# Second attention: queries split per head and 128 tokens, the low part subtracted by GpSimd

## What is computed

```python
def gqa_attend(q, k, v):
    s = jnp.einsum('bkgqd,bksd->bkgqs', q, k, preferred_element_type=jnp.float32) * (HEAD_DIM ** -0.5)
    p = jax.nn.softmax(s, axis=-1).astype(v.dtype)
    return jnp.einsum('bkgqs,bksd->bkgqd', p, v)
...
    o_blocks = lax.map(lambda qb: gqa_attend(qb, k_all, v_all), q_blocks)
...
    o_c = gqa_attend(queries(h_ctx), k_c, v_c)
```

## Time and profile before

| | us |
|---|---|
| median of 3 runs | 3610.65 |
| lowest and highest | 3608.27, 3615.75 |
| the profiled execution, its own time | 3610.93 |
| its span in the trace | 3609.1 |
| TensorE busy | 3254.8 (90%) |
| VectorE busy | 1550.9 (43%) |
| ScalarE busy | 1124.5 (31%) |
| GpSimd busy | 535.9 (15%) |

### The profile page before, as it was taken

The page is one execution under the profiler, slowest core; times in us unless marked ns, Lnnn a source line. Parts: engine busy times, 40 slices in busy tenths (PEclk is TensorE's granted clock), DMA queues, the critical chain, the costliest instruction groups (busy, mean ns, idle before and its releaser), DMA issues. The chain is left out here.

```text
span 3609.1 us, 48582 instructions
## 1 busy us (share of the span) xinstructions
PE 3254.8 (90%) x19154; PEld 2431.0 (67%) x19154; DVE 1550.9 (43%) x2410; ACT 1124.5 (31%) x1679; POOL 535.9 (15%) x394
## 2 busy tenths in 40 slices
PE   7997957999998899988787989999998999899998
PEld 5665611576466687867566778886556888748877
DVE  5644178243224666222655332220006887723332
ACT  4213153142113333233555332220004544422321
POOL 0000022000103343250122220000004322100001
PEclk9998978999999999989798889999997999889999
DMA  3564110121230222211000011111112111112222
GB/s 132 201 250 169 59 38 0 70 95 47 94 128 24 93 94 79 89 66 65 1 1 1 24 47 70 70 47 48 50 68 75 55 69 71 51 67 93 97 84 88
DMA packets 30566, 267.90 MB, mean 74 GB/s; under 512 B 2864, under 2 KB 5296, under 8 KB 10160
## 3 DMA queue, kind: packets, MB, share of 16 engines
q1 hardware_dynamic: 30384, 265.36, 20.0%
HBM read 261.15 MB, written 4.19 MB: 74 GB/s over the span
## 5 line engine op out<-in xcount | busy, mean ns | idle before, releaser
L632 PE MATMUL banks<-normed_high,weights_high 128*128 128x512 f32 (+1 forms) x2264 | 842.0, 379 | 84.6 <-DVEq L455 47.5
L632 PE MATMUL banks<-normed_low,weights_high 128*128 128x512 f32 (+1 forms) x2264 | 831.4, 375 | 0.0
L632 PEld LDWEIGHTS banks<-normed_high,weights_high 128*128 128x128 f32 x2264 | 437.3, 193 | 192.3 <-ACT weights_high L542 41.5
L632 PE MATMUL banks<-normed_high,weights_low 128*128 128x512 f32 (+1 forms) x2264 | 544.5, 371 | 0.0
L263 DVE TENSOR_TENSOR weights_low<-ring,weights_high 128x1024 fp32r<-128x1024 f32 (+1 forms) x194 | 269.5, 1389 | 607.3 <-ACTq L555 539.2
L632 PEld LDWEIGHTS banks<-normed_low,weights_high 128*128 128x128 f32 x2264 | 438.9, 194 | 73.1 <-issue 1.2
L632 PEld LDWEIGHTS banks<-normed_high,weights_low 128*128 128x128 f32 x2264 | 405.2, 191 | 73.7
L553 ACT ACTIVATE weights_high<-ring 128x1024 fp32r<-128x1024 f32 (+1 forms) x226 | 260.9, 1154 | 618.1 <-PE banks L632 452.5
L587 POOL TENSOR_TENSOR latent_total<-latent_total,latent_square 128x512 f32<-128x512 f32 x42 | 77.1, 1836 | 1441.9 <-ACTq L530 1441.9
L632 PE MATMUL banks<-ffn_hidden,ring 128*128 128x256 f32 (+1 forms) x704 | 227.3, 486 | 1.1 <-PEq L154 1.1
L2830 PE MATMUL banks<-normed_high,hg_weights_high 128*128 128x512 f32 (+1 forms) x512 | 190.1, 371 | 15.1 <-DVEq L455 15.1
(11 more groups left out here) (539 smaller groups left out, 4787.9 us busy)
## 6 DMA issues: line engine op xcount, KB each, us to landing
ring<-in_ffn_up SPq DMA_DIRECT2D x33, 2048.0 KB, 7.5
ring<-in_ada SPq DMA_DIRECT2D x48, 1024.0 KB, 6.4
ring<-in_ffn_down SPq DMA_DIRECT2D x24, 1408.0 KB, 5.9
ring<-in_hgrn SPq DMA_DIRECT2D x16, 1536.0 KB, 6.4
ring<-in_gates SPq DMA_DIRECT2D x6, 2048.0 KB, 8.1
ring<-in_wo SPq DMA_DIRECT2D x6, 2048.0 KB, 8.0
ring<-in_w_rw SPq DMA_DIRECT2D x5, 1536.0 KB, 7.5
ring<-in_branch SPq DMA_DIRECT2D x3, 2048.0 KB, 7.8
```

The lines of the kernel that those rows point to most:

```text
L632: mm = pe.matmul(ps[:, 0:y.shape[-1]], w, y, start=(not sweep and kk == 0 and n == 0), stop=(sweep != 0 and kk == kt - 1 and n == len(pair ...
```

## The change

`pa_queries` becomes a ring of 8 pieces, each one head's 128 queries (one unit). ScalarE rounds the piece of unit u+4 in round u, behind its copy of unit u-1, in one 64x128 instruction; it waits until the score of the unit that used the piece's place before is done. GpSimd does the subtraction, also per unit: the pieces of units 0 to 3 first, then the piece of unit u+3 ahead of the probabilities' product of unit u, after its product of unit u-1 has landed. Before the product it waits for its own subtraction. TensorE's score waits for `queries_parted` in every unit. VectorE has nothing to do with the queries any more. `high` and `low` are as before.

```diff
+QUERIES_AHEAD = 4
...
-        QS = k.sb("pa_queries", [P, 2, 2, L], s, F32R)
+        QS = k.sb("pa_queries", [P, 2 * QUERIES_AHEAD, P], s, F32R)
...
+        def queries(u):
+            g, p, j, qt, t, cols, keys = of(u)
+            return Q[rows(p), t, cols.start + qt * P:cols.start + qt * P + P]
...
-                    if qt == 0 and p == 0:
-                        pe.wait_ge(parted.sem, parted.at(j + 1))
+                    pe.wait_ge(parted.sem, parted.at(u + 1))
...
-                    q = QS[:, j % 2, p, qt * P:qt * P + P]
+                    q = QS[:, u % (2 * QUERIES_AHEAD), :]
...
-                def part(j):
...
-                    v.wait_ge(rounded.sem, rounded.at(j + 1))
-                    for p in range(2):
-                        v.tensor_tensor(QS[rows(1 - p), j % 2, p, 0:w], Q[rows(p), t, cols],
-                                        QS[rows(p), j % 2, p, 0:w].bitcast(F32), ALU.subtract).then_inc(e.sem, e.tick())
-                    v.wait_ge(e.sem, e.now())
-                    v.sem_inc(parted.sem, 1)
-                part(0)
-                part(1)
...
-                    if u < n_units and units[u] == (first_group[groups[units[u][0]][0]], 1):
-                        j = groups[units[u][0]][0]
-                        if 1 <= j and j + 1 < n_pairs:
-                            part(j + 1)
...
+                def part(u):
+                    p, x = units[u][1], u % (2 * QUERIES_AHEAD)
+                    g.wait_ge(rounded.sem, rounded.at(u + 1))
+                    g.tensor_tensor(QS[rows(1 - p), x, :], queries(u), QS[rows(p), x, :].bitcast(F32),
+                                    ALU.subtract).then_inc(parted.sem, 1)
+                    g.wait_ge(parted.sem, parted.at(u + 1))
+                for u in range(QUERIES_AHEAD):
+                    part(u)
                 for u in range(n_units):
+                    if u and u + QUERIES_AHEAD - 1 < n_units:
+                        g.wait_ge(normed.sem, normed.at(u))
+                        part(u + QUERIES_AHEAD - 1)
                     x = slice(u % 4, u % 4 + 1)
                     probs = PB[:, u % 3, 0:of(u)[6]]
...
-                def part(j):
...
-                    if j >= 2:
-                        a.wait_ge(scored.sem, scored.at(2 * last_group[j - 2] + 2))
-                    for p in range(2):
-                        a.activation(QS[rows(p), j % 2, p, 0:w], Q[rows(p), t, cols], ACT.Copy).then_inc(e.sem, e.tick())
-                    a.wait_ge(e.sem, e.now())
-                    a.sem_inc(rounded.sem, 1)
+                def part(u):
+                    p, x = units[u][1], u % (2 * QUERIES_AHEAD)
+                    if u >= 2 * QUERIES_AHEAD:
+                        a.wait_ge(scored.sem, scored.at(u - 2 * QUERIES_AHEAD + 1))
+                    a.activation(QS[rows(p), x, :], queries(u), ACT.Copy).then_inc(rounded.sem, 1)
...
-                    if u < n_units and units[u] == (first_group[groups[units[u][0]][0]], 1):
...
+                    if u + QUERIES_AHEAD < n_units:
+                        part(u + QUERIES_AHEAD)
```

12 lines of the change are left out of this document (2 added, 10 removed).

## The result

| | before | after |
|---|---|---|
| median, us | 3611.87 | 3590.15 |
| lowest, highest of the 6 runs after, us | | 3586.78, 3598.61 |
| ratio, with its 95% interval | | 0.9948 (0.9935 to 0.9960) |

The ratio stands for 18.8 us less (14.4 to 23.5); it leaves out one slow run of before (4577.98 us), and likewise one of "before, wide split later" (7833.19). The prediction was 3584.3 us in a range of 3574 to 3602, so 26.3 us less. A second measurement of the same kernel gave 3592.42 us and 0.9950 (0.9931 to 0.9969). The profiled execution of the changed kernel was the longest of its six (3598.61, span 3596.8), so I compare stretches of the stage, not spans.

A forecast was written before the change was run, and what follows sets the result against it. TensorE was taken to set the beat of undisturbed groups. Long pairs 18.4, late products -2, short units 8 and start 1.9 sum to 26.3 us; off the median 3610.65 this gives 3584.3, range 3574 to 3602.

The forecast's parts named there:

- The stop at the queries goes: Long pairs: TensorE's 4.13 us stop behind VectorE's query subtractions disappears; 18.4 us gained over seven pairs.
- The stop that stays at the output's split: Long pairs: VectorE still waits for normed_high before its next maximum; 2.73 us stay per pair, 2.8 with what follows.
- The clock behind it: Long pairs, behind the stop left at the output's split: forecast without the low-clock loss, 3578 to 3591 us, chance 0.50.
- The late products of the even units: Long groups: GpSimd's subtraction ahead of the product makes it some 0.15 us late; 0 to 4 us cost, 2 taken.
- GpSimd's piece: One 64x128 query subtraction on GpSimd takes 0.47 us, bounds 0.29 and 0.73.
- TensorE's extra wait: Each score on TensorE also waits for its own query piece; cost 0.
- Short units: Units with 256 keys: between 3.5 and 15.6 us gained, 8 taken; short pairs of about 7.1 us.
- Start: Start of the stage: first rounding to first score falls from 2.87 to 0.97 us, 1.9 gained.
- the clock rival: Long pairs: a 2.7 us stop also lowers the clock, 7 x 1.4 = 9.8 us less gain, 3594 us; chance 0.20.

The follow-up runs named there:

- before, wide split later: The kernel before, with VectorE's wide query subtractions one round behind ScalarE's roundings, in long pairs only: 3608.63 us, ratio 0.9985.
- normed_low later: VectorE's normed_low issued one round later: in the kernel before 3614.69 us (ratio 1.0007), in the changed kernel 3556.23 us (0.9850).
- both waits taken from before: The kernel before, with the wide subtraction one round later in long pairs and normed_low one round later everywhere: 3586.27 us, ratio 0.9927.
- one experiment here: The changed kernel, with GpSimd's subtraction written behind the product and one piece further ahead, the same instruction list: 3594.17 us, ratio 0.9953.
- the kernel without splits: The kernel before, with the queries of pairs 2 to 15 never split, scores reading the buffers of pairs 0 and 1: 3575.31 us, ratio 0.9898.

## Why the prediction held, and where it didn't

**The stop at the queries goes: right.** No VectorE instruction touches pa_queries, no stop of 4.1 us is left. The stop that stays at the output's split was worked out as 2.73 us; it took 2.92 (2.53 in the first of the seven), because ScalarE's chain ahead of it is 0.2 longer than I took (below).

**The clock behind it: wrong.** The sum took the clock as full behind the stop that stays, with 0.50, and the rival that it stays low with 0.20. The rival is what the trace shows: five of seven pairs are 1.6 us longer, 8.0 in all, where it said 7 x 1.4 = 9.8. The step that failed is the sentence that no row shows a single stop of 2.7 us in a busy stretch. That was a lack of evidence, and I used it as evidence for full clock. The rows of the short stretch, with a clock of 0.67 behind waits of some 0.9 us, pointed the other way, and I gave them too little weight. The trace of before has a nearer case, in the last of the seven pairs, that the prediction doesn't name:

```profile
1930.90 0.90 PE L2397 MATMUL banks<-constants,pa_probs 128*128 128x128 f32 x6 [3.17 <-ACT pa_turned L2531]
...
1933.02 2.47 PE L2413 MATMUL banks<-pa_turned,gq_values 128*64 128x128 f32 x24
```

A stop of 3.17 us, near the predicted 2.73, and the products behind it at the low clock. Had all seven pairs run at full clock, the long stretch would have been 158.86 - 8.0 = 150.9, against 167.63 - 18.4 + 2 = 151.2 predicted.

**The late products of the even units: the size about right, the path half of it.** I took 2 us over 28 groups for a subtraction ahead of the product. The trace has the product late, as predicted: it starts 2.79 us behind the exponential (2.58 in the prediction) and ends at 3.70. But what the transposes waited for was ScalarE's copy, which ends 0.13 us later still. The loss shows in one group of each pair, 0.4 us, 2.8 in all. Both delays hang on the rounding that stands in ScalarE's list, the product's on the subtraction too. The rounding is 0.30 us of work, as predicted, but it lengthens the way from the copy to the exponential by 0.47 (0.49 to 0.96), where I took 0.25. With the subtraction doubled the product comes last and the group grows by 0.4; with the rounding on GpSimd both are in time and the group takes 4.62. No run took away only one of the two delays, so how much of the 0.4 each alone would cost is not shown. The statement "in a long group ScalarE comes to 3.9 us, below 4.63" is true of the sum and missed the path: engines wait for the single copy, not for ScalarE's total.

**GpSimd's piece: right.** 0.47 us predicted from the slope between two shapes, 0.452 measured. **TensorE's extra wait: right.** One wait of the scores for the pieces, at the start of the stage (5.0 us, once), none behind.

**Short units: right,** 8.2 against 8; pairs of them mostly take 6.5 or 7.2 to 8.0 us, 7.1 predicted for all. They too lose to the wait for normed_high: with it gone the stretch is 43.4 instead of 53.7, and the clock 1.00 instead of 0.87.

**Start: right** (2.0 against 1.9). **Two ends left out.** The first pair won 1.1 us, its clock being 0.99 where it was 0.86. The end of the stage lost 2.0: it ran at a clock of 0.67 where it was 1.00. I had put both at nothing without looking at their rows. Of the 2.0, 0.6 is where the cut falls (exponential 95 comes 1.54 us behind 94 instead of 0.91); the rest passes at the lower clock.

**The sum.** 8.8 + 8.2 + 2.0 + 1.1 - 2.0 = 18.1 of 26.3. What is missing is 8.0 for the clock and 0.9 for the two ends, against 0.4 more in the rest of the long pairs and 0.3 in start and short units. Counted with the end of the stage, the short units gained 6.1 us. That the median, 3590.15, lies halfway between the forecast (3584.3) and the clock rival (3594) is not a sign that the truth lies between: the mechanism was the rival's, and that the time still fell in the range is owed to the width of the range.

**The interplay that I didn't see.** The prediction said that the output's split "now stands alone" and left it so. Each of the two waits drains the same pipeline, and what one of them costs depends on the other: moving the output's split in before is worth nothing (ratio 1.0007), the change alone 18.8 us, the two together 54 (0.9850). With the wide pieces kept it is the same: normed_low later brings nothing, the wide split later 5.4 us, both 26. Part of the surplus is the clock, which stays at 1.00 in the long pairs once both waits are gone. In the long pairs neither narrow pieces nor GpSimd are needed for this: both waits taken from before leave 140.1 us. In the short units the pieces help (62.3 without, 43.4 with); a later wide split was not tried there. Which of the two, pieces or the place on GpSimd, makes the short units faster is shown for the kernel with normed_low in its old place: pieces on VectorE leave 53.8, on GpSimd 53.7, so it is the pieces.

**Still open.** Why the clock falls behind some of seven nearly equal stops and not behind others. In the long pairs it repeated in three traces of the same list of instructions, so it depends on more than the stop, but no run here took that apart.

## What to carry to other kernels

Before pricing a wait that goes, look for the next wait on the same engine and price both together: here the one was worth nothing, the other 18.8 us, both 54. Write out the lists of instructions before and after an edit: one experiment here changed the text and not the list. Where an engine waits for another's result in a fixed order, try first to issue the consumer one step later; it took three lines here and brought more on top of the change than the change itself, though nothing without it. When small work is spread evenly over an engine with slack, add it to the longest path through that engine, not to its total.

## What the runs showed of the hardware

The granted clock fell to its lower level behind five of seven stops of 2.5 to 2.9 us in after, behind one of seven of 2.5 in the kernel without splits, behind none of six of 1.5 with both waits gone from before, and in five of the first six pairs with stops of 1.5 and 2.4 us, 6.9 us apart. So the length of a stop alone doesn't tell. Behind such a fall in after the 24 products took up to 2.83 us instead of 1.53, and a pair lost 1.6.

GpSimd rounded a 64x128 piece in 286 ns, no slower than ScalarE (306), and subtracted one in 452 ns with the output on the other 64 partitions, against 300 on VectorE.
